# One block without barriers for all stages, earlier value heads for the second pair, and an output projection that begins with its pooled half

## The chip, the cores and the metric

The kernel runs on one core of a Trainium2 chip. The metric is the device time of one execution in microseconds. Its engines are TensorE (PE; PEld is its weight load), VectorE (DVE), ScalarE (ACT), GpSimd (POOL) and SyncE (SP); each works through its own list of instructions in order, and they wait for each other on semaphores (`wait_ge`, raised by `then_inc`). Transfers (DMAs) are asked for by SyncE, GpSimd or ScalarE, each with its own queue, and are moved by the same 16 DMA engines.

## The reference, cut to what matters

One encoder layer on 1024 tokens of width 1024, in float32:

```
h = rms_norm(x, g_mix);  proj = h @ w_in           # u (512) | q | k | v (512 each) | forget (8)
y_pool = pool_mixer(u, w_pool, pool_scale)          # causal means over 2, 4, 8, 16 tokens, 4 groups of 128
y_attn = forgetting_attention(q, k, v, log_f)       # 8 heads of 64; logits q.k/8 + c_q - c_k, causal softmax
x  = x + concat([y_pool, y_attn]) @ w_out
h2 = rms_norm(x, g_ffn)
logits = h2 @ w_router + b_router; top 4 of 32 experts, softmax gates
x  = x + sum of gate * (clamped_swiglu(h2 @ w_up[e] + b_up[e]) @ w_down[e] + b_down[e])
out = rms_norm(x, g_final)
```

So the contraction of the output projection has a pooled half (the first 512 of 1024) and an attention half, and every later stage needs the sum of both.

## The kernel before

The matrix products up to the router are made of float32 numbers split into a rounded part and a rest: three products (rounded by rounded, rounded by rest, rest by rounded) are added up in PSUM, in matmuls of 128x128 by 512 columns. The program has three blocks, each with a body for each engine; at the end of a block all engines meet in a barrier (it shows in the trace at lines 286, 809 and 1210, where the blocks begin).

**Block 1, projection (line 286).** Tokens are normed and transposed, and v, u, q and k are projected in groups of 128 rows by 512 columns (`s_g` counts the groups: 8 of v, 8 of u, 8 of q, 8 of k). v, q and k go to DRAM (`v_d`, `qk_d`), and are loaded from there again head by head. The weights of a projection and their rests lie in the large buffers weights0 to weights3. GpSimd stores y_pool and loads the value heads 0 and 1; SyncE loads the q and k of heads 0 and 1 between its last stores.

**Block 2, attention (line 809).** Four pairs of heads. A pair is 16 tiles (2 heads by 8 query rows of 128), taken large and small in turn. For a tile TensorE makes logits (lines 963 to 966), VectorE the maxima (900), ScalarE the exponentials (860), TensorE transposes them (974), ScalarE and VectorE copy these out of PSUM (851, 849), and TensorE multiplies with the values (1003) and spreads the row sums (985); VectorE and ScalarE scale, round and take the rest (865, 869, 912, 917; `s_yl` counts the rests, 16 in all). Logits run two to four tiles ahead. `load_qk` (lines 272 to 280) asks for seven pieces of a head: q twice, k twice (each to the lower and the upper 64 rows), q and the rest of k for a second product, and neg_c. SyncE does this for heads 2 and 3, then y_pool and 4 MB of output weights (819), and then for heads 4 to 7, each as soon as the logits of the head that had its place are done (`HEAD_SLOT`; `s_S` counts logits). `load_v` (282 to 284) loads the values of one head; its buffers `VH` are two, so GpSimd asks for a pair's when the products of the pair before are done (line 835; `s_O` counts products). In between ScalarE and VectorE round y_pool and the output weights and take their rests, a quarter at a time (lines 885 to 890 and 937 to 941).

**Block 3, router and experts (line 1210).** SyncE asks for x, g_ffn, x, the router's weights and b_router, and the bias rows (1250 to 1258). TensorE projects (1989 to 1991) token block by token block, each in two halves of 512 columns with 8 steps k of three matmuls: k below 4 take y_pool, the others y_attn. Into the second half it puts the transposes of h2 (2001) of the block's first half, at k from 4 on, and the router's products. VectorE adds x (1620), scales by g_ffn (1627) and chooses the experts; before its first sum it waits for all constants (`s_mc`, line 1655). Then the item table is built, and some 60 items of one expert and up to 160 tokens run in loops to the end. These loops aren't changed.

## Time and profile before

| what | us |
|---|---|
| median of 3 runs | 1929.92 (1928.54 to 1929.95) |
| span of the profiled execution, first to last instruction | 1926.8 |
| TensorE busy | 1839.6 (95%) |
| VectorE busy | 1157.4 (60%) |
| ScalarE busy | 884.2 (46%) |
| GpSimd busy | 255.7 (13%) |
| mean granted clock of TensorE | 0.982 |

The page gives no time of its own for the profiled execution beside its span. The stages in the trace: projection until 219, attention from 221 to 370, output projection and router until about 490, the item table until about 515, and the experts to the end. Busy time is an average over all of them. A row of a timeline gives the start, the duration, the engine, the line, what is written and read, and in brackets how long the engine had been idle and what ended that.

### The profile page before, as it was taken

The page shows a single profiled execution, that of the slowest core. Times are in us where ns is not written, and L with a number is a line of the kernel's source. Part 1 is how long each engine was busy: PE and PEld are TensorE (multiplying, and loading weights), DVE is VectorE, ACT ScalarE, POOL GpSimd, SP SyncE. Part 2 cuts the span into 40 slices and gives each one's busy share as a digit, 9 for nine tenths or more (in the row PEclk, how much of TensorE's full clock was granted, in tenths as well). Part 3 has the DMA queues.
Part 4 walks back from the last instruction along what each step waited for, and adds up shares of the span by engine and source line. Part 5 has one row for each costly group of instructions (what it writes and reads, how often), then busy time and mean ns, then how long its engine had stood idle before and what let it go on. Part 6 is the DMA issues. An engine that isn't in the chain of part 4 may idle for free.

```text
span 1926.8 us, 33268 instructions
## 1 busy us (share of the span) xinstructions
PE 1839.6 (95%) x12118; PEld 1552.5 (81%) x12118; DVE 1157.4 (60%) x1695; ACT 884.2 (46%) x1212; POOL 255.7 (13%) x216
## 2 busy tenths in 40 slices
PE   8999978899599999999999999999999999999995
PEld 6777767688488888888888788888888889998884
DVE  5343356423799999999999944444444444334446
ACT  4312356432677777777777633333333322222234
POOL 0000000000211221222122111111111111111100
PEclk9999989999699999999999999999999999999998
DMA  5223773232699999999999988888888888777773
GB/s 198 73 82 130 199 205 78 64 120 98 255 407 387 362 372 355 375 365 357 378 364 361 363 287 284 284 284 284 285 284 285 286 286 287 260 270 268 260 255 147
DMA packets 176257, 507.98 MB, mean 264 GB/s; under 512 B 13704, under 2 KB 14344, under 8 KB 159746
## 3 DMA queue, kind: packets, MB, share of 16 engines
q1 hardware_dynamic: 159074, 457.65, 64.7%
q0 software_dynamic: 16000, 47.31, 8.6%
q10 hardware_dynamic: 1120, 2.16, 0.4%
q8 instruction: 42, 0.69, 0.2%
q14 instruction: 21, 0.17, 0.0%
HBM read 469.29 MB, written 46.33 MB: 268 GB/s over the span
## 4 chain that ended last, share of the span: by engine, by line
PE 75%; DVE 2%; DMA 1%; issue 1%; ACT 0%; DVEq 0%; POOL 0%; SPq 0%; ACTq 0%; POOLq 0%
PE ps L2096 26%; PE ps L2157 18%; PE ps L2238 6%; PE ps L2132 3%; PE ps L2245 3%; PE ps L2106 3%; PE ps L2133 3%; PE ps L2139 3%; PE ps L2078 2%; PE ps L1989 2%; PE ps L1991 1%; PE ps L1990 1%; PE ps L2145 1%; PE ps L2220 1%; DMA xg_rows<-h2g_d,row_index_next 1%
## 5 line engine op out<-in xcount | busy, mean ns | idle before, releaser
L2096 PE MATMUL ps<-xg,weights 128*128 128x132 f32 (+4 forms) x4096 | 503.7, 285 | 3.0 <-DVE xg L1242 0.8
L2096 PEld LDWEIGHTS ps<-xg,weights 128*128 128x128 f32 x4096 | 497.5, 190 | 9.5 <-issue 9.5
L1842 DVE TENSOR_TENSOR weights_r<-weights,w_rounded 128x2048 fp32r<-128x2048 f32 x192 | 432.1, 2284 | 1.0 <-ACT w_rounded L1496 0.7
L1496 ACT ACTIVATE w_rounded<-weights 128x2048 fp32r<-128x2048 f32 x192 | 359.5, 1921 | 55.5 <-DVE weights_r L1842 27.2
L1370 POOL DMA_INDIRECT acc_d<-y_rows,row_index_now x62 | 111.8, 1803 | 798.0 <-ACT y_rows L1480 435.2
L1790 DVE TENSOR_TENSOR weights_r<-weights,w_down_rounded 128x1024 fp32r<-128x1024 f32 x128 | 148.0, 1218 | 28.9 <-PE ps L2110 28.9
L1346 POOL DMA_INDIRECT xg_rows<-h2g_d,row_index_next x64 | 109.6, 1712 | 337.6 <-DVE row_index_next L1773 203.8
L2157 PE MATMUL ps<-w_rounded,x_rounded 128*128 128x512 f32 x512 | 151.3, 397 | 0.0
L2157 PE MATMUL ps<-w_rounded,x_rest 128*128 128x512 f32 x512 | 148.8, 392 | 0.0
L1804 DVE TENSOR_SCALAR glu<-ps,b_up_t 128x132 f32<-128x132 f32 (+4 forms) x128 | 38.0, 359 | 174.8 <-PE ps L2096 174.8
L2157 PE MATMUL ps<-weights_r,x_rounded 128*128 128x512 f32 x512 | 129.9, 396 | 0.0
L1461 ACT ACTIVATE glu_sigmoid<-glu 128x528 f32<-128x528 f32 (+4 forms) x32 | 21.7, 678 | 226.3 <-DVE glu L1804 226.3
L1452 ACT ACTIVATE w_down_rounded<-weights 128x1024 fp32r<-128x1024 f32 x128 | 124.2, 1041 | 0.0
L2157 PEld LDWEIGHTS ps<-weights_r,x_rounded 128*128 128x128 f32 x512 | 96.2, 188 | 22.6
L2157 PEld LDWEIGHTS ps<-w_rounded,x_rest 128*128 128x128 f32 x512 | 96.7, 189 | 21.4
L2132 PE MATMUL ps<-w_down_rounded,hidden_r 128*128 128x512 f32 x256 | 113.5, 443 | 0.3 <-DVE hidden_rest L1796 0.3
L2157 PEld LDWEIGHTS ps<-w_rounded,x_rounded 128*128 128x128 f32 x512 | 95.8, 189 | 20.9
L1809 DVE TENSOR_SCALAR lin<-ps,b_up_t 128x132 f32<-128x132 f32 (+4 forms) x128 | 37.9, 358 | 110.4 <-PE ps L2096 109.5
L2133 PE MATMUL ps<-w_down_rounded,hidden_rest 128*128 128x512 f32 x256 | 100.6, 393 | 0.0
L1456 ACT ACTIVATE hidden_r<-hidden 128x512 fp32r<-128x512 f32 x32 | 20.2, 631 | 164.0 <-DVE hidden L1818 164.0
L680 PE MATMUL ps<-h_t_r,weights_r 128*128 128x512 f32 x192 | 77.8, 405 | 0.0
L681 PE MATMUL ps<-h_t_rest,weights_r 128*128 128x512 f32 x192 | 76.2, 397 | 0.0
(315 smaller groups left out, 2866.7 us busy)
## 6 DMA issues: line engine op xcount, KB each, us to landing
weights<-in_w_up SPq DMA_DIRECT2D x128, 2048.0 KB, 10.4
weights<-in_w_down SPq DMA_DIRECT2D x64, 2048.0 KB, 12.0
weights<-in_w_in SPq DMA_DIRECT2D x3, 2048.0 KB, 8.4
xt<-in_x SPq DMA_DIRECT2D x8, 512.0 KB, 4.2
qk_d<-stage_rounded SPq DMA_DIRECT2D x16, 256.0 KB, 2.5
qk_d<-stage_rest SPq DMA_DIRECT2D x16, 256.0 KB, 2.8
q_stack<-qk_d SPq DMA_DIRECT2D x16, 256.0 KB
k_stack<-qk_d SPq DMA_DIRECT2D x16, 256.0 KB
```

Source lines behind the costliest of these rows:

```text
L680: pe.matmul(o, w(k), hT_r[:, k, tok], start=(k == 0), stop=False)
L1346: pool.indirect_dma_start(out=rows[b][0:BLK[b], :], out_offset=None, in_=h2g_d, in_offset=bass.IndirectOffsetOnAxis(ap=ixn[0:BLK[b], b:b + ...
L1370: pool.indirect_dma_start(out=acc_d, out_offset=bass.IndirectOffsetOnAxis(ap=ixc[0:BLK[b], b:b + 1], axis=0), in_=yr[b][0:BLK[b], :], in_o ...
L1452: act.activation(quarter(whi[c - 4], q), quarter(raw[c], q), ACT.Copy).then_inc(s_wa, 1)
L1496: ins = act.activation(wh[SLOT[j]][:], src, ACT.Copy)
L1790: dve.tensor_tensor(quarter(raw_r[c], q), quarter(raw[c], q), quarter(whi[c - 4], q).bitcast(F32), ALU.subtract).then_inc(s_wb, 1)
L1842: ins = dve.tensor_tensor(piece_of(raw_r, j)[1], piece_of(raw, j)[1], wh[SLOT[j]][:].bitcast(F32), ALU.subtract)
L2096: last = pe.matmul(o, raw[c][:, k, t * P:(t + 1) * P], xg[:, k, 0:w], start=(k == 0), stop=(k == KT - 1))
L2132: pe.matmul(psum[2 * (c % 2)][:], uh[:, k, :], whi[c - 4][:, k, :], start=(k == 0), stop=False)
L2133: pe.matmul(psum[2 * (c % 2)][:], ul[:, k, :], whi[c - 4][:, k, :], start=False, stop=False)
L2157: return pe.matmul(psum[bank][:], x, w, start=start, stop=stop)
L2238: last = pe.matmul(psum[2 * half][:], u[:, k, :], w, start=(u is uh and k == 0), stop=False)
```

## The change

What it does, apart from the indentation of the bodies:

1. The three blocks become one. Every engine runs its three bodies one after the other, without a barrier. What a barrier had guaranteed is waited for by name: TensorE waits for the last q/k rest and the last pooled output before the first logits; SyncE for y_pool's stores before heads 2 and 3; GpSimd and, ahead of the bias rows, SyncE for the last rest of y_attn (`s_yl`).
2. There are four value buffers in place of two. The new two lie in the second quarter of weights0. GpSimd asks for the values of heads 2 and 3 when the 16th group after u's start (the last of q) is done, for those of heads 4 and 5 after the first pair's products, for those of heads 6 and 7 after the third pair's. ScalarE waits for the second pair's products (`s_O` at 16) before it rounds weights into that quarter.
3. `load_qk` is cut into `load_q` (three pieces) and `load_k` (four pieces). For head 7 SyncE asks for the q part and GpSimd for the k part, on the same condition, and TensorE waits for both.
4. SyncE asks for g_ffn when the logits of head 6 are done, for the router's constants when all logits are done, for x when all transposes of probabilities are done. These constants are counted on `s_c2`.
5. The output projection of token block 0 makes k from 0 to 3 of both halves first, then waits for `s_yl`, and then makes k from 4 to 7 of both. The other blocks are as before.

The diff, with the re-indentation and renamed semaphores left out:

```diff
-        VH = [m.take(f"v_head{i}", [P, NT, HD], F32, at=pout_at + 4 * NT * HD * i) for i in range(2)]
+        VH = [m.take(f"v_head{i}", [P, NT, HD], F32, at=(pout_at if i < 2 else raw_at + 4 * 2 * CW) + 4 * NT * HD * (i % 2))
+              for i in range(4)]
...
-        def load_qk(sp, h, s):
+        def load_q(eng, h, s):
             q = bass.ds(h * HD, HD)
             for part in range(2):
-                sp.dma_start(QS[s][part * HD:(part + 1) * HD].bitcast(F32), qk_d[0, part, q]).then_inc(s_ld[s], 16)
+                eng.dma_start(QS[s][part * HD:(part + 1) * HD].bitcast(F32), qk_d[0, part, q]).then_inc(s_ld[s], 16)
+            eng.dma_start(QA[s][0:HD].bitcast(F32), qk_d[0, 0, q]).then_inc(s_ld[s], 16)
+
+        def load_k(eng, h, s, landed):
+            q = bass.ds(h * HD, HD)
             for part in range(2):
...
+                eng.dma_start(KS[s][part * HD:(part + 1) * HD].bitcast(F32), qk_d[1, 0, q]).then_inc(landed, 16)
+            eng.dma_start(KA[s][0:HD].bitcast(F32), qk_d[1, 1, q]).then_inc(landed, 16)
+            eng.dma_start(KA[s][HD:QK_ROWS].bitcast(F32), negc_d[bass.ds(h, 1)].rearrange("h a s -> (h a) s")).then_inc(landed, 16)
...
                 for head in range(2):
                     load_v(pool, head, head)
+                pool.wait_ge(s_g, N_Q + 8)
+                for head in range(2, 4):
+                    load_v(pool, head, head)
...
-        with nc.Block() as block:
             @block.sync
...
+                sp.wait_ge(s_ps[1], 16 * NG // 2)
                 for head in range(2, 4):
-                    load_qk(sp, head, HEAD_SLOT[head])
+                    load_q(sp, head, HEAD_SLOT[head])
+                    load_k(sp, head, HEAD_SLOT[head], s_ld[HEAD_SLOT[head]])
...
                     sp.wait_ge(s_S[1], 8 * (before // 2) + 7 + before % 2)
-                    load_qk(sp, head, HEAD_SLOT[head])
+                    load_q(sp, head, HEAD_SLOT[head])
+                    if head < NH - 1:
+                        load_k(sp, head, HEAD_SLOT[head], s_ld[HEAD_SLOT[head]])
...
-                for j in range(1, NH // 2):
+                pool.wait_ge(s_O, 8)
                     for h2 in range(2):
-                        pool.wait_ge(s_O, 8 * j)
-                        load_v(pool, 2 * j + h2, h2)
+                    load_v(pool, 4 + h2, h2)
+                pool.wait_ge(s_S[1], 8 * 2 + 7)
+                load_k(pool, NH - 1, HEAD_SLOT[NH - 1], s_lv[2])
+                pool.wait_ge(s_O, 24)
+                for h2 in range(2):
+                    load_v(pool, 6 + h2, h2)
...
+                        if m == 6:
+                            act.wait_ge(s_O, 16)
                         act.wait_ge(s_wo[m % 2], 16)
...
                 pe.wait_ge(s_on, 4)
+                pe.wait_ge(s_ql, GRP - N_Q)
+                pe.wait_ge(s_pe, 2 * NG)
...
                         pe.wait_ge(s_ld[s], head_loads(n))
+                        if head_of(n) == NH - 1:
+                            pe.wait_ge(s_lv[2], 16 + 64)
...
+                    buffers, loads = ((0, 1), (2, 1), (0, 2), (0, 3))[g // 4]
                     if g % 4 == 0 and kind == 0:
                         for h2 in range(2):
-                            pe.wait_ge(s_lv[h2], 16 * (g // 4 + 1))
+                            pe.wait_ge(s_lv[buffers + h2], 16 * loads)
...
-        with nc.Block() as block:
...
             @block.sync
             def _(sp):
+                sp.wait_ge(s_S[1], 8 * 3 + 7)
+                sp.dma_start(gfr[:], g_ffn.to_broadcast([P, D])).then_inc(s_c2, 16)
+                sp.wait_ge(s_S[1], 8 * 4)
+                sp.dma_start(wr[:], w_router[0].rearrange("(k p) e -> p k e", p=P)).then_inc(s_c2, 16)
+                sp.dma_start(brr[:], b_router.to_broadcast([P, NE])).then_inc(s_c2, 16)
+                sp.wait_ge(s_T, banks_until(TILES - 1))
                 for i in range(NT):
...
                     if i == 1:
+                        sp.wait_ge(s_yl, GROUPS)
...
             @block.gpsimd
             def _(pool):
+                pool.wait_ge(s_yl, GROUPS)
...
-                dve.wait_ge(s_mc, 64)
+                dve.wait_ge(s_c2, 64 + 48)
...
             @block.tensor
             def _(pe):
-                pe.wait_ge(s_yl, GROUPS)
-
-                def out_proj(i, half, between):
+                def out_proj(i, half, between, ks=range(KT)):
...
-                    for k in range(KT):
+                    for k in ks:
...
-                    last.then_inc(s_og, 1)
+                    if k == KT - 1:
+                        last.then_inc(s_og, 1)
...
-                for i in range(NT):
-                    out_proj(i, 0, second_half(i - 1) if i >= 1 else lambda k: None)
+                pe.wait_ge(s_ol, 3 * NH // 2)
+                for half in range(2):
+                    out_proj(0, half, lambda k: None, range(4))
+                pe.wait_ge(s_yl, GROUPS)
+                out_proj(0, 0, lambda k: None, range(4, KT))
+                out_proj(0, 1, first_half_and_route(0), range(4, KT))
+                for i in range(1, NT):
+                    out_proj(i, 0, second_half(i - 1))
                     out_proj(i, 1, first_half_and_route(i))
```

## Rows read from the trace of the kernel before

**Rows 1.** The head of the profile page.
```profile
span 1926.8 us, 33268 instructions
```
**Rows 2.** Busy time by stage: window, its length, engines (x instructions), PEclk, DMA share, GB/s.
```profile
515.00:1926.80 1411.80, 1386.45 (x9327) 1187.98 (x9326) 927.99 (x1231) 678.75 (x790) 226.10 (x133) 0.99 0.86 313
```
**Rows 3.** Waits of PE, 200 to 384 us: total, times, longest.
```profile
PE ps L1003 <- DMA v_head<-v_d: 9.7, 1, 9.7
```
**Rows 4.** Timeline: values of the second pair, request and first use.
```profile
256.31 1.75 POOL L284 DMA_DIRECT2D v_head<-v_d  x2 [29.56 <-PE ps L1003]
...
271.20 3.39 PE L1003 MATMUL ps<-prob_t_big,v_head 128*64 128x128 f32 x32 [9.70 <-DMA v_head<-v_d]
...
275.19 0.98 PE L974 MATMUL ps<-ident,prob_big 128*128 128x128 f32 x7
```
**Rows 5.** Timeline of SP: store of q's last rounded group.
```profile
174.38 0.32 SPq L326 DMA_DIRECT2D qk_d<-stage_rounded  x1
```
**Rows 6.** Transfers: the value loads' landing times, and b_router's issue (last: us to landing).
```profile
DMA to landing us min/median/max: 3.7/4.1/13.9
...
b_router_row<-in_b_router SPq DMA_DIRECT2D x1, 16.0 KB, 8.6
```
**Rows 7.** Timeline of PE: the same place in pair three.
```profile
305.56 1.97 PE L1003 MATMUL ps<-prob_t_big,v_head 128*64 128x128 f32 x32 [0.57 <-ACT prob_t_big L851]
...
308.11 0.98 PE L974 MATMUL ps<-ident,prob_big 128*128 128x128 f32 x7
```
**Rows 8.** Short windows, columns as in rows 2.
```profile
248.00:250.00 2.00, 2.00 (x15) 1.37 (x14) 1.22 (x2) 2.00 (x5) 0.00 (x0) 1.00 1.02 382
...
264.00:266.00 2.00, 0.00 (x0) 0.00 (x0) 0.00 (x0) 0.04 (x1) 0.00 (x0) 0.50 1.02 209
...
328.00:329.00 1.00, 0.00 (x0) 0.00 (x0) 0.37 (x1) 1.00 (x3) 0.00 (x0) 1.00 1.13 225
```
**Rows 9.** Timeline around the barrier of line 809.
```profile
219.18 0.69 DVE L423 SCALAR_TENSOR_TENSOR stage_rest<-ps,stage_rounded 128x512 fp32r<-128x512 f32 x1 [4.91 <-ACT stage_rounded L419]
...
220.82 0.47 PE L963 MATMUL ps<-k_stack,q_stack 128*128 128x512 f32 x1 [2.30 <-PEq L286]
```
**Rows 10.** Timeline: head 7's loads and wait, and the same piece one pair earlier.
```profile
293.38 0.71 PE L974 MATMUL ps<-ident,prob_big 128*128 128x128 f32 x5
...
299.88 1.09 PE L974 MATMUL ps<-ident,prob_big 128*128 128x128 f32 x8
...
321.13 1.09 SPq L275 DMA_DIRECT2D q_stack<-qk_d  x2
...
326.28 0.71 PE L974 MATMUL ps<-ident,prob_big 128*128 128x128 f32 x5
330.76 0.50 PE L963 MATMUL ps<-k_stack,q_stack 128*128 128x512 f32 x1 [3.76 <-DMA k_rest_and_neg_c<-negc_d]
...
336.88 1.09 PE L974 MATMUL ps<-ident,prob_big 128*128 128x128 f32 x8
```
**Rows 11.** Timeline around the barrier of line 1210 and the first token block.
```profile
367.74 0.61 PE L985 MATMUL ps<-ident,row_sum_inv 128*64 128x128 f32 x8
...
369.72 0.42 DVE L917 TENSOR_TENSOR y_attn_lo<-y_scaled,y_attn_hi 128x256 fp32r<-128x256 f32 x1 [0.48 <-ACT y_attn_hi L869]
...
370.61 0.47 PE L1989 MATMUL ps<-weights_r,y_pool_hi 128*128 128x512 f32 x1 [2.26 <-PEq L809]
...
380.89 0.69 DVE L1620 TENSOR_TENSOR x<-ps,x_res 128x512 f32<-128x512 f32 x1 [10.75 <-DMA b_router_row<-in_b_router]
...
382.36 0.33 PE L2001 MATMUL ps<-ident,h_row 128*128 128x128 f32 x1 [2.50 <-DVE h_row L1627]
...
387.21 0.39 PE L1989 MATMUL ps<-weights_r,y_pool_hi 128*128 128x512 f32 x1
...
389.29 0.27 PE L2001 MATMUL ps<-ident,h_row 128*128 128x128 f32 x1
...
392.52 0.40 PE L1989 MATMUL ps<-weights_r,y_pool_hi 128*128 128x512 f32 x1
```

More of the change, by code:

```diff
@@ L1002, in product @@
                         for h2 in range(2):
[L1003 removed]
+                            last = pe.matmul(psum[7][h2 * HD:(h2 + 1) * HD, c:c + P], VH[buffers + h2][:, k, :],
                                              prob_t(first + 2 * h2)[:, k, :], start=(k == 0), stop=(k == qi))
@@ new lines, in build @@
+            thr = m2.take("count_steps", [NE, NFULL + len(WIDTHS) - 1], F32)
+            ecol = m2.take("expert_col", [NE, 1], F32)
+            s_dc = sem("disp_consts")
+            s_dl = sem("disp_landed")
+            BIGI = 4096
+            DISP_CONSTS = 8 + NFULL + len(WIDTHS)
+            xr = [m.take(f"x_res{i}", [P, D], F32) for i in range(2)]
+            x2 = [m.take(f"x2_{i}", [P, D], F32) for i in range(4)]
+            h2r = [m.take(f"h2_row{i}", [P, D], F32) for i in range(4)]
@@ new lines, in build @@
+            sqd = m.take("x2_square_dump", [P, D], BF16)
+            rst2 = m.take("x2_rstd", [P, NT], F32)
+            gsum = m.take("gate_sum", [P, NT, 2], F32)
+            ohe = m.take("one_hot", [P, TOPK, NE], F32)
+            gall = m.take("gates_dense", [P, NT, NE], F32)
+            ioe = m.take("iota_e", [P, NE], F32)
+            s_io = sem("iota_e_set")
+            s_xr = [sem(f"x_res_landed{i}") for i in range(2)]
+            s_og = sem("out_proj_done")
+            s_x2 = sem("x2_done")
@@ new lines, in build @@
+            s_bh = sem("b_down_rounded")
+            s_hs = [sem(f"h2_stored{i}") for i in range(4)]
+            s_as = [sem(f"acc_stored{i}") for i in range(4)]
+            s_tb = sem("item_table_done")
+            s_bt = sem("bias_tables_done")
+            RV = 6
+            m = phase()
+            m.end = mix_at
+            posm = m.take("position", [P, NT, NE], F32)
+            tab = m.take("item_table", [P, ITEMS], I32)
+            tbf = m.take("item_base", [P, ITEMS], F32)
+            nit = m.take("class_last", [NE, NCLS + 2], I32)
@@ new lines, in build @@
+            uh_at = m.at
+            uh = m.take("hidden_r", [P, KT, P], F32R)
+            assert m.at <= yp_at
+            m.at = yp_at
+            rows_at = m.at
+            rows = [m.take(f"xg_rows{b}", [P, ROW], F32) for b in range(2)]
+            dump = m.take("final_dump", [P, D], BF16, at=rows_at)
+            sel = m.take("select", [P, NT, 2 * P], BF16)
+            pcol = m.take("position_col", [P, NT], BF16)
+            selx = m.take("expert_select", [P, P], F32R)
+            selu = m.take("expert_select_up", [P, P], F32R)
@@ new lines, in build @@
+            s_ix = sem("index_done")
+            s_rw = [sem(f"rows{b}_landed") for b in range(2)]
+            s_xt = sem("x_transposed")
+            s_xe = [sem("xg_even_done"), sem("xg_odd_done")]
+            s_gn = sem("gate_next_done")
+            s_cur = sem("index_gate_now")
+            s_evd = sem("up_evacuated")
+            s_eva = sem("down_evacuated")
+            s_sg = sem("sigmoid_done")
+            s_tm = sem("glu_lin_done")
+            s_hf = sem("hidden_done")
+            s_ua = sem("w_up_rounded")
```

478 lines of the change are left out of this document (207 added, 271 removed).

## The prediction

> **What bounds the kernel now.** I read the page first for the span, 1926.8 us [rows 1], then the busy time by stage. From 515 us to the end TensorE is busy for 1386 of 1412 us at a granted clock of 0.99 [rows 2]: the expert stage is a solid block, this change doesn't touch it, and it starts when the item table is ready, so whatever is won earlier slides it forward one for one. The room lies in the attention stage and at its two edges. The view of waits for TensorE between 200 and 384 us is led by one hole of 9.7 us, for the value heads of the second pair [rows 3]. The chain of waits is no help before 370 us (it runs out at SyncE's first request after the second barrier), so the rest I read from the timeline around lines 809 and 1210, where the barriers are.
>
> **Part 1, value heads of pair two (heads 2 and 3).** Before, GpSimd asks for them at 256.31, after the last product of pair one, because both use the two `VH` buffers; by then 4 MB of output weights, y_pool and heads 4 and 5 fill the DMA engines, and TensorE stands from 261.50 to 271.20 [rows 4]. After, they have buffers of their own in a quarter of weights0 and are asked for when the q projection is done. That is shortly before SyncE stores its last rounded group at 174.38 [rows 5], some 87 us before they are needed, while an undisturbed value load lands in about 4 us (its median) [rows 6]. So this wait goes entirely. What is late next: pair two's first product then waits as pair three's does, 0.57 us for ScalarE's copy of the transposed probabilities. In pair three that start (304.99, its 305.56 less the wait) to the next transposes (308.11) takes 3.12 us [rows 7]; in pair two the same piece takes 275.19 - 261.50 = 13.69 us [rows 4]. The difference, 10.57, is the term: 9.70 of wait and the rest matmuls behind the hole (32 of them took 3.39 us against 1.97 in pair three), where the granted clock was at 0.50, the 1.2 GHz level, as it stands for 264 to 266 [rows 8]. I take **10.6 us**, bounds 9.7 (the wait alone) and 11.3 (with the 0.57 and a little more gone). Heads 4 and 5 now use the old buffers one product earlier and have a whole pair of time. ScalarE's new wait, that pair two's products are done before it overwrites this quarter, comes at tile 37, when TensorE has already passed tile 32: behind it would be queued all of ScalarE's exps, but it is met before it is reached, so nothing. Its y_pool and weight rounding inside the attention loop isn't moved.
>
> **Part 2, the first barrier (line 809).** VectorE's last remainder starts at 219.18 and lasts 0.69, so it is done at 219.87; TensorE's first logits start at 220.82 [rows 9]. The new wait on that same remainder, in place of the barrier, leaves about 0.08 of hand-over: **0.9 us**, bounds 0 (heads 0 and 1 were the true wait) and 1.0. ScalarE's table load of 1.28 us, seen right behind the barrier, moves ahead under the projection. SyncE's loads of heads 2 and 3 don't come earlier, since the waits for the last stores stay in front of them.
>
> **Part 3, head 7.** SyncE asked for the seven pieces from 321.13 on, and TensorE resumed at 330.76 after 3.76 us of standing still, 9.63 us after the first request [rows 10]. After, the four K pieces go through GpSimd's queue and the three q pieces through SyncE's, on the same release. The prize: from the transposes at 326.28 to those at 336.88 is 10.60 us, the same piece one pair earlier (293.38 to 299.88) 6.50 [rows 10], so 4.1 us for the wait with the lower clock after it. But the issue isn't what binds: six pieces of 256 KB at 225 GB/s, the rate in 328 to 329 with the DMA share at 1.13 [rows 8], are 7.0 of the 9.63 us. From below: GpSimd's later start could make the K pieces later; each of its loads takes 3.7 to 4.1 us to land undisturbed and 13.9 at worst [rows 6], the worst under a far longer backlog than this, so I bound the loss at 1.5. From above: the whole 4.1. I take **1.0 us**, near the row of the DMA rate, for the requests that come out sooner and the shorter hole. One rule bears on this. The rows show 64-row pieces at 225 GB/s and the 128-row output weights at 382 (248 to 250) [rows 8]. The Trainium skill, "SBUF — State Buffer", section "Door 1: The DMA port swizzle (why `[64,N]` ≈ `[32,N]`)", says that 64 partitions reach only half of the memory's DMA ports, and the trace agrees; its section "Can I just issue two DMAs to hit both halves?" says that two concurrent transfers to the two halves gained only 6%. By that rule an estimate for this part is 0.4 us (6% of 7.0) and the sum would be 17.4 in place of 18.0.
>
> **Part 4, the second barrier, the router's constants and the pooled half.** Before, TensorE's last attention instruction ends at 368.35 (367.74 and 0.61), VectorE's last remainder at 370.14 (369.72 and 0.42), the output projection starts at 370.61. VectorE can't take its first result: it stands until 380.89 for b_router, which SyncE asked for only after the barrier and which lands 8.6 us after issue [rows 6, 11]. TensorE, which wants VectorE's h_row for its first transpose, stops at 379.86 and resumes at 382.36. After: the constants are asked for while the last logits run, and x when the last transposes are done, all before 367; by the 8.6 us they land before 376. TensorE goes at 368.35 straight into the 24 matmuls of the two pooled halves (half the contraction, four k of three matmuls, twice): 5.6 us, which covers VectorE's end at 370.14, so the wait on it costs nothing. At 39 matmuls between 370.61 and 379.86 (less the 0.40 of the last) the pace is 0.233. The order is new: the first 512 columns are complete only at the 36th matmul: 368.35 + 35 x 0.233 + 0.40 = 376.9. Residual and scaling then take 1.5 (380.89 to 382.36), so the first transpose comes at 378.4 instead of 382.36: 3.9 us. TensorE, done with its 39 at 377.5, waits 0.9 us for it, where it used to have four k of the other half for cover. The second gain is the clock: behind the 2.50 us hole the piece of four transposes and twelve matmuls from 382.36 to 387.21 takes 4.85 us, at full clock (389.29 to 392.52) 3.23: 1.6 us [rows 11]. A hole of 0.9 is like the 0.57 in pair three [rows 7], after which the matmuls keep their pace. Together **5.5 us**; bounds 3.9 (the clock still falls) and 5.8. SyncE's bias rows and GpSimd's constants now wait for the last remainder, as they did at the barrier; the item table wants them 100 us later.
>
> **Sum.** 10.6 + 0.9 + 1.0 + 5.5 = 18.0 us. From the span, 1926.8, that is 1908.8. The median of the runs, 1929.92, lies 3.1 above that span; the page gives no own time for the profiled execution, so I carry the 3.1 along: **1911.9 us**. The ends: 9.7 + 0 - 1.5 + 3.9 = 12.1, so 1917.8; 11.3 + 1.0 + 4.1 + 5.8 = 22.2, so 1907.7.
>
> **Rivals.** A: the split of head 7 removes its wait (two queues move their halves side by side). For it: the pieces alternate between the lower and upper 64 rows, and a 128-row transfer did go at 382 GB/s. Against: the DMA share was already full on one queue. 18.0 - 1.0 + 4.1 = 21.1: 1908.8 us. Chance 0.2. B: the K pieces on GpSimd's queue become the later ones, and the clock still falls at the output projection, so those terms come to -1.5 and 3.9: 10.6 + 0.9 - 1.5 + 3.9 = 13.9: 1916.0 us. For it: 13.9 us to land has been seen; against: that backlog isn't there. Chance 0.12. C: the value wait goes but is taken over by the next thing from the same backlog, heads 4 and 5, whose requests stand behind the output weights. It would give back at most the 10.6: 1922.5 us. Against: pair three's first logits stood just ahead of 293.38 [rows 10], so I expect TensorE there at about 280, when the queue that held the value heads up until 271 should have run dry. Chance 0.05. D, the slower side: the long expert stage at a lower granted clock. Its matmuls are nearly back to back, so a mean of 0.98 for its 0.99 is 14 us on 1412; from 0.977 on it eats the whole gain, and 0.97 would give 1911.9 + 28 = 1940 us. Against it: the clock fell only behind holes of 2.5 us and more [rows 4, 10, 11], and the change makes none there. Chance 0.03. That the change doesn't do what it says (the explicit waits rebuild the barriers exactly): the parts 2 and 4 would be near 0, 1918.3; chance 0.03, since the wait on the last remainder is now behind 24 matmuls.
>
> **Numbers.** Forecast 0.57 with 1911.9, its own range 1909.5 to 1915; A 0.2, B 0.12, C 0.05, D 0.03, the last 0.03. For 8 in 10 I take **1907.5 to 1917**, which holds the forecast, A and B. What can be told from no change is about 0.2%, 3.9 us. C and the last rival stay faster by more than that, so faster 0.95; same 0.02 (half-measures of D); slower 0.03.
>
> **What would show it.** In the profile after: no wait of the first value product of pair two above 1 us, and a granted clock near 1.00 around it; logits starting within 0.2 us of the last remainder; the wait for head 7 between 2.5 and 4 us (forecast), under 1 (A) or above 4.5 (B); projection matmuls on y_pool that start as the last scale spread ends; VectorE's first residual released by TensorE, not by DMA, and a TensorE hole of about 0.9 behind it. I am wrong if a new wait above 2 us stands between 220 and 370, or if the stretch from the item table to the end isn't 1412 us within 2.

## The result, and the profile after

| | before | after |
|---|---|---|
| median of runs, us | 1929.78 (1928.54 to 1929.95, 4 runs) | 1912.03 (1911.08 to 1913.18, 4 runs) |
| span of the profiled execution, us | 1926.8 | 1911.1 (its own time 1913.18) |
| mean granted TensorE clock | 0.982 | 0.986 |

The ratio is 0.9909 (95% interval 0.9895 to 0.9923). The forecast was 1911.9. The spans differ by 15.7 and the medians by 17.75, because the profiled execution of after was the slowest of its four and lies 2.1 above its span, where I had carried 3.1 over from before. So the steps have to be held against the 15.7.

The stretch that the change doesn't touch is the window to the end, which answers to [rows 2] (columns: window, its length, busy time of PE, PEld, DVE, ACT, POOL, the granted clock, DMA share, GB/s). The clock is at 0.99 again, and the head of the page gives the span. The window begins some 16 us further into the work than it did before, so its length can't be compared by itself. The first expert's bias matmul can: it starts at 514.17 before and at 498.27 after, and from there to the end it is 1412.63 and 1412.83 us, within the 2 us that the prediction asked for.

```profile
span 1911.1 us, 33247 instructions
```
```profile
515.00:1911.10 1396.10, 1370.14 (x9258) 1174.35 (x9256) 913.89 (x1221) 667.51 (x784) 215.25 (x126) 0.99 0.85 312
```
```profile
514.17 1.19 PE L2157 MATMUL ps<-bias_table,expert_select_up 128*128 128x512 f32 x2 [4.50 <-DVE x_rest L1830]
...
498.27 1.19 PE L2185 MATMUL ps<-bias_table,expert_select_up 128*128 128x512 f32 x2 [4.15 <-DVE x_rest L1855]
```

Next, PE's waits between 200 and 384 us (what waits, for what: total, times, longest), which answer to [rows 3]. The 9.7 for the value heads is gone, and what leads is the wait for head 7, which has grown. At the bottom stands the new small one, for `h_row`.

```profile
PE ps L984 <- DMA q_and_ones<-qk_d: 4.3, 1, 4.3
PE ps L995 <- DVE prob_t_big L864: 2.3, 3, 1.3
...
PE ps L2023 <- DVE h_row L1652: 1.0, 1, 1.0
```

The timeline of the value heads of pair two, POOL's request first, answers to [rows 4]. The request is 87 us ahead of its use; 0.58 for ScalarE's copy is what is left of the hole; the 32 matmuls take 1.97 us and not 3.39.

```profile
173.77 1.76 POOL L288 DMA_DIRECT2D v_head<-v_d  x2 [15.64 <-PE ps L690]
...
261.00 1.97 PE L1025 MATMUL ps<-prob_t_big,v_head 128*64 128x128 f32 x32 [0.58 <-ACT prob_t_big L866]
...
263.55 0.98 PE L995 MATMUL ps<-ident,prob_big 128*128 128x128 f32 x7
```

Where the barrier of line 809 stood [rows 9], VectorE's last remainder ends at 219.63 and the logits start 0.10 later.

```profile
218.94 0.69 DVE L431 SCALAR_TENSOR_TENSOR stage_rest<-ps,stage_rounded 128x512 fp32r<-128x512 f32 x1 [4.91 <-ACT stage_rounded L427]
...
219.73 0.47 PE L984 MATMUL ps<-k_stack,q_stack 128*128 128x512 f32 x1 [1.46 <-issue]
```

Head 7, against [rows 10]: SP's first request for q, POOL's for K, the last transposes ahead of the hole, the resume, and the transposes behind it. From first request to resume it is 10.14 us, where it was 9.63.

```profile
309.54 1.08 SPq L276 DMA_DIRECT2D q_stack<-qk_d  x2
...
309.80 1.09 POOL L282 DMA_DIRECT2D k_stack<-qk_d  x2 [52.82 <-PE ps L987]
...
314.68 0.71 PE L995 MATMUL ps<-ident,prob_big 128*128 128x128 f32 x5
...
319.68 0.76 PE L984 MATMUL ps<-k_stack,q_stack 128*128 128x512 f32 x1 [4.28 <-DMA q_and_ones<-qk_d]
...
326.36 0.87 PE L995 MATMUL ps<-ident,prob_big 128*128 128x128 f32 x6
```

Where the barrier of line 1210 stood, against [rows 11]: the last scale spread, the projection right behind it (before VectorE's last remainder, 359.18), VectorE's first residual, now released by PE, and the first transpose.

```profile
357.20 0.61 PE L1006 MATMUL ps<-ident,row_sum_inv 128*64 128x128 f32 x8
357.73 0.50 PE L2010 MATMUL ps<-weights_r,y_pool_hi 128*128 128x512 f32 x1
...
359.18 0.43 DVE L934 TENSOR_TENSOR y_attn_lo<-y_scaled,y_attn_hi 128x256 fp32r<-128x256 f32 x1 [0.48 <-ACT y_attn_hi L884]
...
366.53 0.69 DVE L1645 TENSOR_TENSOR x<-ps,x_res 128x512 f32<-128x512 f32 x1 [6.92 <-PE ps L2012]
...
368.00 0.33 PE L2023 MATMUL ps<-ident,h_row 128*128 128x128 f32 x1 [0.99 <-DVE h_row L1652]
...
371.29 0.39 PE L2010 MATMUL ps<-weights_r,y_pool_hi 128*128 128x512 f32 x1
```

**The account by pieces.** Each is the length between two landmarks before, less that after:

| piece | before | after | gain | forecast |
|---|---|---|---|---|
| last q projection matmul starts (218.12, 217.88) | | | 0.24 | 0 |
| that matmul to the first logits | 2.70 | 1.85 | 0.85 | 0.9 |
| transposes ahead of pair two's values to those behind (from 256.37, from 255.29) | 18.82 | 8.26 | 10.56 | 10.6 |
| transposes to transposes over head 7's hole | 10.60 | 11.68 | -1.08 | +1.0 |
| last scale spread to first `h_row` transpose | 14.62 | 10.80 | 3.82 | 3.9 |
| transposes and twelve matmuls behind it | 4.85 | 3.29 | 1.56 | 1.6 |
| all the rest | | | -0.25 | 0 |

The sum is 15.7; of the rest, -0.20 is the expert stage (1412.63 against 1412.83). One step of the forecast has the wrong sign: the split of head 7.

### The profile page after: what moved, and what is told of

Same layout as the page of the kernel before. It is cut to its first block, busy times and chain, and to the rows that moved or that the text cites. A ratio compares the mean times of both kernels' runs of the same rounds, so it can differ in the third digit from the quotient of the medians.

```text
span 1911.1 us, 33247 instructions
## 1 busy us (share of the span) xinstructions
PE 1836.1 (96%) x12118; PEld 1549.0 (81%) x12118; DVE 1157.6 (61%) x1695; ACT 884.4 (46%) x1212; POOL 255.2 (13%) x220
## 4 chain that ended last, share of the span: by engine, by line
PE 92%; DVE 3%; DMA 2%; issue 1%; ACT 1%; DVEq 0%; POOL 0%; SPq 0%; ACTq 0%; POOLq 0%
PE ps L2124 26%; PE ps L2185 18%; PE ps L2266 6%; PE ps L2160 3%; PE ps L2273 3%; PE ps L2167 3%; PE ps L2134 3%; PE ps L2161 3%; PE ps L688 2%; PE ps L690 2%; PE ps L689 2%; PE ps L995 2%; PE ps L2010 2%; PE ps L1025 2%; PE ps L2106 2%; PE ps L2012 2%
```

## The experiments

All have the changed kernel as their base, except the first. "Spread" is a `row_sum_inv` matmul group, "hole" PE's idle time just ahead of head 7's first logits, and "piece" is from the transposes ahead of it to those behind it (10.60 before, 11.68 after).

**values_only.** The kernel before with Part 1 alone; both barriers, head 7 on one queue and the order of the projection stay.

```diff
-        VH = [m.take(f"v_head{i}", [P, NT, HD], F32, at=pout_at + 4 * NT * HD * i) for i in range(2)]
+        VH = [m.take(f"v_head{i}", [P, NT, HD], F32, at=(pout_at if i < 2 else raw_at + 4 * 2 * CW) + 4 * NT * HD * (i % 2))
+              for i in range(4)]
...
+                pool.wait_ge(s_g, N_Q + 8)
+                for head in range(2, 4):
+                    load_v(pool, head, head)
```

> The kernel before with one thing of the change: four value buffers, and the values of heads 2 and 3 asked for once q is projected. All barriers stay. Theory (the terms of the forecast are independent and each is what its piece of the timeline says): the 9.7 us wait and the slow matmuls behind it go, 10.6 us off the time before, about 1919.2 us, head 7's wait stays at 3.8 us, the hole of 2.5 us before the first h2 transpose stays. Rival (the barriers are what makes the stages long, the value wait is covered by the next transfer of the same backlog): at most 3 us off, 1927 or more.

Measured: 1920.5 us (1917.59 to 1922.11, 4 runs), ratio 0.994 (0.9923 to 0.9957), against 1931.12 for the kernel before on that chip: 10.6 less. The hole for the values is gone, both barriers stand (2.30 and 2.27 us of idle PE), the `h_row` hole is 2.47. In its trace the piece from the transposes ahead of pair two's values to those behind is 8.21 us where before had 18.82: 10.61. So the values' term stands alone; the trace says so more sharply than the medians, whose interval is 8.3 to 14.9. But head 7's piece, with nothing of the split in it, was 11.96 us and not 10.60, and from the first logits to the first spread it was 12.60 where before had 10.59. Both are taken up below.

**late_values.** The changed kernel with heads 2 and 3 asked for after the last product of pair one, in their own buffers; a single run.

```diff
-                pool.wait_ge(s_g, N_Q + 8)
-                for head in range(2, 4):
-                    load_v(pool, head, head)
...
                 pool.wait_ge(s_O, 8)
+                for head in range(2, 4):
+                    load_v(pool, head, head)
```

> The changed kernel, with the values of heads 2 and 3 in their own buffers but asked for only when the first pair's products are done, ahead of those of heads 4 and 5. Theory (the wait comes from the request's place behind the backlog of output weights and heads, not from the buffers): the wait of about 9.7 us is back (8.7 to 11), clock at 0.5 in it, 10 to 11.5 us more than the changed kernel, about 1922.5 us. Rival (removing barriers or sharing the queue had already shortened the landing): under 5 us of wait.

Measured: 1924.35 us. The hole is back, with the backlog (timeline, whose last row has only those 20 of the 32 matmuls that lie in the stretch looked at; then a window in the hole):

```profile
257.60 3.50 POOL L288 DMA_DIRECT2D v_head<-v_d  x4 [30.92 <-PE ps L1024]
...
271.88 2.40 PE L1024 MATMUL ps<-prob_t_big,v_head 128*64 128x128 f32 x20 [9.07 <-DMA v_head<-v_d]
```
```profile
268.00:270.00 2.00, 0.00 (x0) 0.00 (x0) 0.00 (x0) 0.00 (x0) 0.00 (x0) 0.50 1.07 223
```

The request at 257.60 was waited for until 271.88, 14.3 us, with the DMA share at 1.07. The piece from transposes to transposes is 19.02 us, as long as before's 18.82. (A further 2.0 us of this run's time is the clock at the first logits, taken up at the end.) The gain of Part 1 comes from the time of asking, not from having the buffers.

**one_queue.** Head 7's four K pieces back on SP's queue; what TensorE waits for is counted accordingly.

```diff
-                    if head < NH - 1:
-                        load_k(sp, head, HEAD_SLOT[head], s_ld[HEAD_SLOT[head]])
+                    load_k(sp, head, HEAD_SLOT[head], s_ld[HEAD_SLOT[head]])
...
-                pool.wait_ge(s_S[1], 8 * 2 + 7)
-                load_k(pool, NH - 1, HEAD_SLOT[NH - 1], s_lv[2])
```

> The changed kernel with head 7's k pieces back on SyncE's queue behind its q pieces, nothing else undone. Theory (splitting the request over two queues moves no byte faster and lets the q_and_ones piece, which TensorE also needs, land later): the wait for head 7 goes from 4.3 back to about 3.8 us and the clock falls for a shorter time behind it, 1.1 us less from the transposes before the wait to those of the last pair, so about 0.5 to 1.1 us off the changed kernel: 1911.0 us. Rival (the longer wait is chance of that one execution): wait 4.3, time 1912.0.

Measured: 1913.61 us (1912.03 to 1915.03, 4 runs), ratio 0.9908 (0.9891 to 0.9924). The hole is 3.71 us and the resume 9.56 us after the first request, both shorter than after's, but the piece is 11.90: the clock was low for longer behind it (7.48 us from the resume to the transposes, against 6.68). The median was expected at 1911.0; it missed that by 2.6.

**opposite_halves.** Head 7's K pieces in the other order, so that each queue begins with another 64 rows.

```diff
-            for part in range(2):
+            for part in ((1, 0) if h == NH - 1 else (0, 1)):
```

> The changed kernel, with GpSimd asking for head 7's two k_stack pieces in the other order (upper 64 rows first), so that it writes to other rows than SyncE's queue at the same time. Theory (two transfers of 64 rows at once are no faster than one after the other): rate stays at 210 to 230 GB/s, wait for head 7 between 3.9 and 4.6 us, time 1912.0 within 0.7. Rival (the two queues only met on the same half): the rate goes towards 385 GB/s, the wait to 2 us or less, the clock doesn't fall, time 1908 to 1909.

Measured: 1913.53 us (1911.04 to 1914.84, 4 runs), ratio 0.9905 (0.9888 to 0.9921); hole 4.20, piece 12.13, the rate 209 GB/s in the window from 319 to 320, with the DMA share at 1.06. The median is 1.5 above what was expected, but 0.1 from one_queue's on the same chip. Which half each queue begins with makes no difference that could be told here.

**wide_loads.** The scratch tensor laid out by heads, so that the two parts of q, and of K, are one transfer of 128 rows: five transfers per head on one queue in place of seven, for head 7 too. The stores are twice as many and half as large.

```diff
-        qk_d = nc.dram_tensor("qk_d", [2, 2, AW, S], F32).ap()
+        qk_d = nc.dram_tensor("qk_d", [2, NH, 2, HD, S], F32).ap()
...
-            for part in range(2):
-                eng.dma_start(QS[s][part * HD:(part + 1) * HD].bitcast(F32), qk_d[0, part, q]).then_inc(s_ld[s], 16)
+            eng.dma_start(QS[s][:].bitcast(F32), qk_d[0, h].rearrange("a r s -> (a r) s")).then_inc(s_ld[s], 16)
...
```

> The changed kernel with head 7 on SyncE's queue alone, and q and k stored so that the stack of a head is 128 rows in one piece: q_stack is (q rounded, q rest) and k_stack (k rest, k rounded), one load of 128 rows each, the second product takes q rounded and k rounded. The same products are summed in another order; five loads for a head in place of seven, the same bytes; the stores are in pieces of 64 rows. Theory (a load into 64 rows goes at 225 GB/s, into 128 rows at 385): a head is 4 x 256 KB at 385 and 2 x 256 KB at 225, 5.0 us in place of 7.0; the wait for head 7 falls from 3.8 to about 1.8 us and the clock stays, so 2.0 to 3.3 us off one_queue: about 1908.2 us. Rival (the rate is set by something else than the rows of the destination, as the reads from DRAM): 225 GB/s for all, wait 3.8, time 1911.

Measured: 1910.04 us (1908.0 to 1911.0, 4 runs), ratio 0.9887 (0.9871 to 0.9904). Two rows show it, the resume and a short window in the load:

```profile
318.56 0.62 PE L976 MATMUL ps<-k_stack,q_stack 128*128 128x512 f32 x1 [2.70 <-DMA k_rest_and_neg_c<-negc_d]
```
```profile
315.00:316.00 1.00, 0.86 (x8) 0.55 (x6) 1.00 (x3) 0.41 (x1) 0.00 (x0) 1.00 1.14 401
```

The hole is 2.70 us, first request to resume 8.56, and the piece 9.45. In the fastest window the same engines move 401 GB/s; with 64-row pieces the windows behind the first of a load had 188 to 250 at a share of 0.95 and more. The gain is smaller than expected (a hole of 1.8 and a clock that stays up): the granted clock reads 0.50 from 319 to 322. And the DMA engines are no longer full: in the five us from 2.5 us behind the first request the share is 0.73, where it was 1.01 to 1.06 with 64-row pieces, and SP's request for the K stack alone takes 2.29 us. So something other than the engines holds the last piece now; which, no run separates. one_queue had 1913.61 on this chip, but 2.1 us between the two traces lie at the first logits, where the clock fell in one_queue's only; the piece is the better measure.

**after_again and one_queue_again.** The two earlier medians, 1912.03 and 1913.61, weren't taken side by side (the kernel before had 1929.78 beside the one and 1931.12 beside the other), and the traces disagreed with them: so both kernels ran once more, on one chip. The edit of the second is that of one_queue; the first has none.

> The changed kernel once more, on the same chip as the next two, as their yardstick. Expected: its median of 1912.0 within 1. At the first logits the earlier profiles show two courses: in some the clock falls to 0.50 for some 5 us and the piece from the first logits to the first scale spread is 12.6 us long, in others it doesn't and the piece is 10.6. Both theories expect this kernel to spread over about 2 us for that reason.

> Head 7's K and q pieces all on SyncE's queue, as before the change, everything else as changed. Theory 1 (the split makes the last piece 0.5 us later, and what the clock does behind the hole has nothing to do with the queue): the median is the changed kernel's within 1 us, the hole 3.7 to 3.9 us against 4.2 to 4.3, first request to resume 9.6 to 9.8 us against 10.1. Theory 2 (the earlier medians, 1913.6 against 1912.0, are an effect of the split): this one is slower than the changed kernel by 1 to 2 us.

Measured: the split 1913.38 us (1912.27 to 1914.8, 4 runs), ratio 0.9908 (0.9891 to 0.9924); one queue 1912.24 (1910.19 to 1914.07, 4 runs), ratio 0.9901 (0.9885 to 0.9918). The intervals overlap widely: no difference can be told, and the first pair had the sign the other way. How far one kernel's executions differ is in the next rows of one_queue_again, the same code as one_queue:

```profile
315.63 0.71 PE L990 MATMUL ps<-ident,prob_big 128*128 128x128 f32 x5
...
320.00 0.77 PE L979 MATMUL ps<-k_stack,q_stack 128*128 128x512 f32 x1 [3.66 <-DMA k_rest_and_neg_c<-negc_d]
...
326.09 1.09 PE L990 MATMUL ps<-ident,prob_big 128*128 128x128 f32 x8
```

One kernel's piece was 11.90 in one execution and 10.46 in the other, with holes of 3.71 and 3.66. Only the time behind the resume differs, 7.48 and 6.09. Windows of 1 us show the granted clock at 0.50 from 322 to 328 in the first (0.85 in the one ahead, 0.73 in the one behind), and in the second at 0.53, 0.50, 0.50 and 0.77 from 320 to 324 only. Over all traces with loads of 64 rows and the hole unfilled:

| | traces | transposes to resume | resume to transposes | piece |
|---|---|---|---|---|
| one queue | 4 | 4.37 to 4.64 | 6.12, 7.32, 7.48, 6.09 | mean 11.23 |
| two queues | 7 | 4.83 to 5.04 | 6.62 to 7.40 | mean 11.90 |

The first column is the split's own effect, 0.46 us to the bad on the means (4.94 less 4.48), with no overlap. The second is the clock's. Two of the four traces on one queue had the short course of some 6.1 us and none of the seven on two queues; in the changed kernel the clock is at 0.50 already from 318, inside the hole, and in before it is at 1.00 until 332, behind the resume at 330.76. Whether the later resume makes the long course more likely, or this is chance, is not shown.

The split also changes the kind of queue: the profile calls SP's queue hardware and GpSimd's software. In all seven traces the same bytes took the DMA engines longer on GpSimd's (in after, window 309 to 321; packets, MB, share of 16 engines):

```profile
q0 software_dynamic: 272, 0.79, 32.2%
q1 hardware_dynamic: 240, 0.79, 27.8%
```

No run gave the K pieces to a second queue of the first kind. So whether the 0.46 us comes of having two queues or of this queue stays open.

**keep_busy.** Sixteen 128x512 matmuls on head 6's stacks in the hole, into the bank that head 7's first logits overwrite; nothing of them is used.

```diff
+                        if n == 50:
+                            pe.wait_ge(s_P[0], n // 2 - 1)
+                            six = HEAD_SLOT[NH - 2]
+                            for _ in range(16):
+                                pe.matmul(logits_at(n)[:, 0:512], QS[six][:, 0:P], KS[six][:, 0:512],
+                                          start=True, stop=True)
```

> The changed kernel, with 16 matmuls of 128x512 on head 6's stacks in the hole ahead of head 7's first logits, into the bank that these overwrite; they compute nothing that is used. 16 x 0.235 is 3.8 us, which fills most of the 4.3 us hole; the pieces land when they land. Theory 1 (half of what the wait for head 7 costs is the lower clock behind the hole): the granted clock stays at 1.00 through the stretch, the piece from the resume to the scale spread, 6.1 to 6.5 us with the split, comes down to about 3.5, and the median is 2 to 3 us below the changed kernel's. Rival (the clock falls anyway, or the lower clock hides no path): within 0.7 us of it.

Measured: 1910.6 us (1909.48 to 1911.62, 4 runs), ratio 0.9897 (0.988 to 0.9913), 2.8 below after_again on the same chip; the runs of the two don't overlap. Its timeline, and the window at the resume:

```profile
314.97 3.89 PE L978 MATMUL ps<-k_stack,q_stack 128*128 128x512 f32 x16
319.38 0.47 PE L990 MATMUL ps<-k_stack,q_stack 128*128 128x512 f32 x1 [0.53 <-DMA q_and_ones<-qk_d]
...
323.87 1.09 PE L1001 MATMUL ps<-ident,prob_big 128*128 128x128 f32 x8
```
```profile
319.00:320.00 1.00, 0.62 (x3) 0.57 (x4) 0.00 (x0) 0.00 (x0) 0.00 (x0) 1.00 0.00 0
```

The pieces still land 10.03 us after the first request, but the clock is at 1.00 throughout and resume to transposes is 4.49 us against 6.62 to 7.40. In the changed kernel the same window reads 0.50:

```profile
319.00:320.00 1.00, 0.32 (x1) 0.35 (x2) 0.00 (x0) 0.11 (x1) 0.00 (x0) 0.50 0.00 0
```

So of the 11.9 us of the piece, 2.1 to 2.9 are the clock behind the hole. The wait itself is only part of its price.

**whole_sum_first and one_pooled_half.** The order of the output projection: the first without a pooled half ahead of the wait for the last remainder, the second with the first column half's pooled part alone ahead of it.

```diff
-                for half in range(2):
-                    out_proj(0, half, lambda k: None, range(4))
                 pe.wait_ge(s_yl, GROUPS)
-                out_proj(0, 0, lambda k: None, range(4, KT))
-                out_proj(0, 1, first_half_and_route(0), range(4, KT))
+                out_proj(0, 0, lambda k: None)
+                out_proj(0, 1, first_half_and_route(0))
```
```diff
-                for half in range(2):
-                    out_proj(0, half, lambda k: None, range(4))
+                out_proj(0, 0, lambda k: None, range(4))
                 pe.wait_ge(s_yl, GROUPS)
                 out_proj(0, 0, lambda k: None, range(4, KT))
-                out_proj(0, 1, first_half_and_route(0), range(4, KT))
+                out_proj(0, 1, first_half_and_route(0))
```

> The changed kernel, with the output projection of token block 0 in the order of before: it waits for the last remainder of y_attn and then makes the first 512 columns whole, then the others. Theory (the pooled halves first cover the 2 us until the remainder, but take away the four k of the other half that covered VectorE's sum, and open a hole of 1.0): the first matmul 1.9 us later, no hole before the first transpose, which comes 0.8 us later than in the changed kernel (11.6 us after the start of the last scale spread in place of 10.8): 1912.8 us. Rival (the pooled halves are worth their cover, 1.9 us, or the hole stays): 1914.

> The changed kernel, but only the pooled part of the first 512 columns goes ahead of the wait for the last remainder; then the rest of these columns, then the other 512 in one. Theory: 12 matmuls (2.8 us) cover the 1.9 us until the remainder, the first 512 columns are whole after 24 matmuls, and VectorE's sum and scaling run beside the pooled part of the others, so no hole: the first transpose comes after 39 matmuls, 1.0 us earlier than in the changed kernel (9.8 us after the start of the last scale spread): 1911.0 us. Rival (VectorE isn't ready, since x or the router's constants land too late for the earlier sum): a wait on a DMA and 1912 or more.

Measured, on one chip: 1912.46 us (1912.05 to 1913.41, ratio 0.9911, 0.9894 to 0.9927) and 1910.67 (1910.45 to 1912.77, ratio 0.9904, 0.9887 to 0.992), 4 runs each. From the last spread to the first `h_row` transpose it is 11.63 and 9.65 us, against 10.80 as changed. The first row is of whole_sum_first, the two others of one_pooled_half:

```profile
360.26 0.47 PE L2010 MATMUL ps<-weights_r,y_pool_hi 128*128 128x512 f32 x1 [1.94 <-DVE y_attn_lo L934]
```
```profile
363.79 0.69 DVE L1645 TENSOR_TENSOR x<-ps,x_res 128x512 f32<-128x512 f32 x1 [4.15 <-PE ps L2012]
...
366.89 0.27 PE L2023 MATMUL ps<-ident,h_row 128*128 128x128 f32 x1
```

Without a pooled half PE waits 1.94 us for VectorE; with both, it waits 0.99 for `h_row`, since the first 512 columns are ready late; with one, it waits for neither. Twelve matmuls (2.8 us) already cover VectorE's last remainder.

**late_constants.** x, g_ffn, w_router and b_router asked for after the last remainder, in the order of before; a single run.

```diff
-                sp.wait_ge(s_S[1], 8 * 3 + 7)
-                sp.dma_start(gfr[:], g_ffn.to_broadcast([P, D])).then_inc(s_c2, 16)
...
-                sp.wait_ge(s_T, banks_until(TILES - 1))
+                sp.wait_ge(s_yl, GROUPS)
```

> The changed kernel, with x, g_ffn, the router's weights and b_router asked for as before, one after the other, only when the last remainder of y_attn is done. No barrier. Theory (the hole of 2.5 us and the lower clock behind it come from the late request, not from the barrier): VectorE's first sum is released by b_router some 10.5 us after the last remainder, the first transpose follows 1.5 us later, about 14.5 us after the start of the last scale spread in place of 10.8; the hole is about 4.7 us since TensorE started earlier, and the granted clock falls behind it: 5 to 6 us more than the changed kernel from the spread to the third block's first matmul, about 1917.5 us. Rival (the barrier made most of it): 1 to 2 us more.

Measured: 1917.1 us. It is one execution, 4.6 us above whole_sum_first and 6.4 above one_pooled_half on the same chip. SP asks for b_router at 362.03, VectorE is let go at 370.46, and the hole is 4.35 us with the granted clock at 0.50 from 373 to 375:

```profile
370.46 0.69 DVE L1643 TENSOR_TENSOR x<-ps,x_res 128x512 f32<-128x512 f32 x1 [10.30 <-DMA b_router_row<-in_b_router]
...
371.94 0.33 PE L2021 MATMUL ps<-ident,h_row 128*128 128x128 f32 x1 [4.35 <-DVE h_row L1650]
```
```profile
373.00:375.00 2.00, 2.00 (x8) 1.51 (x7) 0.00 (x0) 0.00 (x0) 0.00 (x0) 0.50 0.03 8
```

Spread to first transpose is 14.18, near the 14.62 of before. Without the early requests, taking away the barrier and reordering the projection would have brought 0.4 us here. Which of the early requests counts, that for x or those for the constants, was not separated; the last to land was b_router.

**wide_half_busy.** The three that helped together: wide_loads, one_pooled_half, and ten filling matmuls as in keep_busy.

> The best version by the rows so far: loads of 128 rows on one queue, one pooled half ahead of the wait instead of two, and ten 128x512 matmuls (2.35 us) on head 6's stacks in the hole ahead of head 7, which compute nothing that is used. If the three add up: 1910.0 (the wide loads) less 1.2 (third residual 18.4 us behind the spread instead of 19.6) less 1.6 (the 5.5 us behind the hole become 3.95 at full clock) is 1907.2 us, ratio to the kernel before about 0.987; hole ahead of head 7 about 0.4 us with the clock at 1.00. If the hole and the order of the projection already hide behind each other, or something new is late, it stays at 1909 or above.

Measured: 1907.62 us (1906.86 to 1908.85, 4 runs), ratio 0.9885 (0.9869 to 0.9902). Piece 7.92, spread to first transpose 9.66:

```profile
319.22 0.50 PE L982 MATMUL ps<-k_stack,q_stack 128*128 128x512 f32 x1 [0.40 <-DMA k_rest_and_neg_c<-negc_d]
...
364.25 0.27 PE L2021 MATMUL ps<-ident,h_row 128*128 128x128 f32 x1
```

In the traces the three add up: against wide_loads the filling takes 1.53 us off the piece at head 7 and the order of the projection 1.15 off the spread to the first transpose. The median is the fastest seen and within 0.4 us of the 1907.2 expected, but that closeness is not evidence: the kernel before was 1.3 faster on this chip than on wide_loads's, and against it the gain is 22.2 us where wide_loads had 21.1 (ratio 0.9885, expected 0.987). The intervals of the ratios overlap, with the changed kernel's too.

## Why the prediction was right, and where it was wrong

**Part 1 held** in its size (10.56 for 10.6) and in its two halves, the wait and the clock behind it. values_only gave the same 10.6, in its trace and in the medians. Rival C, that heads 4 and 5 would then be late, is out: between 261 and 294 PE's longest waits are 0.58.

**Part 2 held**: 0.85 for 0.9. The hand-over that I put at 0.08 was 0.10.

**Part 3 failed.** The step was that the requests come out sooner and the hole shortens by 1.0 us. The first half happened: the last of the seven was asked for 1.84 us after the first (311.38, K, against 309.54), where it was 4.04 us before. But the last piece didn't land sooner. The DMA engines were full on one queue (share 1.05, 227 GB/s over the five us from 2.5 us behind the first request) and not faster on two (213 to 220 in the seven traces; the four on one queue had 220 to 227), and the last piece came later: 9.96 to 10.19 us after the first request, against 9.53 to 9.78. I had named this limit myself, and then took a gain from the issue all the same. The estimate after the Trainium skill, "SBUF — State Buffer", section "Can I just issue two DMAs to hit both halves?" (6%, 0.4 us gained), was nearer, and still too high: here the rate fell by some 3%, and the last piece landed 0.5 us later. Why two queues move less isn't shown. Rival A (hole under 1 us) is out. B came near, in size (-1.5 for -1.08) and in part in its mechanism: GpSimd's last K piece, asked for at 311.38, landed 8.2 us later, at 319.58, which is 10.04 us after the first request where everything was there after 9.63 before; but the piece that TensorE waited for was a q piece, `q_and_ones` on SP's queue, just behind it. The remaining 0.6 of the 1.08 can't be laid to the split: in before's profiled execution the low clock cost little (6.12 us behind the resume; the same work with one queue took 7.32 in values_only, 7.48 in one_queue and 6.09 in one_queue_again). My price of 4.1 us for this wait was read from that one execution.

What would have paid is in the same section of the prediction, unused: 64-row pieces at 225 GB/s and 128-row ones at 382 [rows 8]. wide_loads turned that into 1.1 us less of waiting than on one queue.

**Part 4 held** (3.82 and 1.56 for 3.9 and 1.6), with the hole at 0.99 where I said 0.9, and the clock staying up. late_constants shows which part of it carries: the early requests for x and the constants. The prediction took the pooled halves as one step; one of the two was worth more than both, by 1.15 us.

**The sum** was 18.0 by steps against 15.7 in the spans: 2.1 too much in Part 3, 0.2 in the others and the rest. The median was met to 0.1 only because a second error made up for this one: I carried 3.1 from the span to the median, and after's median lies 0.9 above its span. Elsewhere an execution's own time lies 1.8 to 2.1 above its span, so before's profiled execution was one of its fastest, some 1928.8 (an estimate from its span and these). That closeness is luck; the 15.7 against 18.0 is the better measure of the forecast. Rival D (the expert stage at a lower clock) didn't come: 0.99 in both. Nor did the last rival; the barriers are gone and stay gone.

## What to carry to other kernels

When the DMA engines are already full, don't expect a load split over two queues to land sooner; here its last piece came 0.5 us later. Look at the DMA share and at the rows per transfer before you look at the issue, and make the transfers wide. Price a hole on TensorE as the hole plus what the clock costs behind it, and read that from more than one execution, since one trace showed 6.1 us and the next 7.5 for the same work. Where a hole can't be closed, matmuls that compute nothing can keep the clock up, and where an engine must be covered, cover it with just enough work, because more delays what the next engine wants.

## What the runs showed of the hardware

The granted clock doesn't follow a hole strictly. Between the q projection and the first logits PE is idle for 1.46 us (2.30 with the barrier), and for some 0.5 to 1.1 a few matmuls later. The second of these isn't what brings the clock down: in one_queue the granted clock reads 0.86 from 222 to 223 and 0.50 in the next, and that idle time ends at 224.49. In 10 of the 14 traces the clock stayed at 1.00 and the first logits to the first spread took 10.6 us; in 4 (values_only, one_queue, opposite_halves, late_values) it went to the 1.2 GHz level and the same piece took 12.6 to 12.7. Here is one window of the changed kernel, and the same of one_queue:

```profile
224.00:228.00 4.00, 3.96 (x30) 3.31 (x29) 2.70 (x7) 2.92 (x8) 1.89 (x2) 1.00 0.49 127
```
```profile
224.00:228.00 4.00, 3.52 (x15) 3.02 (x15) 1.79 (x3) 2.48 (x7) 1.89 (x2) 0.50 0.29 79
```

PE executes 30 matmuls against 15 in 4 us, for the same code behind the same hole of 1.46 (one_queue is 0.96 us earlier in its work there). So 2.0 us come and go with this place alone, and up to 1.4 more at head 7. A third place is as large: from the first expert's bias matmul to the end, in code that no run changes, the 14 traces take from 1410.54 us (one_queue) to 1413.18 (one_queue_again). The runs of one kernel spread by 1.4 to 4.5 us, and these three are large enough for it; executions without a trace can't be asked, so how much each makes of it isn't shown. A difference of 1 or 2 us between two medians of four runs is therefore read from the pieces of the traces, and not from the medians alone. What decides in one execution whether the clock falls stayed open.

A 64-row piece and a 128-row one keep the DMA engines equally busy: the share was 1.12 at 246 GB/s in one window of one_queue_again and 1.14 at 401 in wide_loads. So the share says how long the engines are occupied, not how much they move. For the whole of head 7's load (1.58 MB, windows of 12 us) they were occupied for 5.1 us in wide_loads and for 6.8 to 7.3 in the four traces with 64-row pieces on one queue.

Not tried: giving head 7 the slot that head 3 leaves free two pairs earlier. The output weights' rounding writes into that memory while head 7's logits run, so it would need the rounding moved as well.
